# Opening of a two-block transformer kernel: the load of x moved to the head of SyncE's queue, and seven of the sixteen modulation pieces multiplied by TensorE instead of one

## The reference

```
c_act = silu(c)                                  # 1024 numbers
mod   = c_act @ w_ada + b_ada                    # w_ada is 1024 x 9216
sh1, sc1, g1, sh2, ... = split(mod, 9)
u = rmsnorm(x, norm_ff1) * (1 + sc1) + sh1
h = x + 0.5 * g1 * (silu(u @ w_gate) * (u @ w_up)) @ w_down
```

## Time and profile before

| | |
|---|---|
| median of 3 runs | 1648.84 us (1647.54 to 1648.98) |
| the profiled execution | 1650.04 us |
| its span | 1648.4 us |
| TensorE busy | 1624.7 us, 99% |
| VectorE, ScalarE, GpSimd busy | 1155.3, 799.2, 172.4 us |
| mean DMA rate | 191 GB/s |

### The profile page before, as it was taken

How to read it: one execution, slowest core, us unless ns; L and a number is a source line. 1 busy time by engine, 2 the same in 40 slices (tenths; PEclk the granted TensorE clock), 3 DMA queues, 4 the chain that set the end, 5 groups by cost and what they waited for, 6 DMA issues and landing times.

```text
span 1648.4 us, 33761 instructions
## 1 busy us (share of the span) xinstructions
PE 1624.7 (99%) x13615; PEld 1586.4 (96%) x13615; DVE 1155.3 (70%) x1449; ACT 799.2 (48%) x973; POOL 172.4 (10%) x193
## 2 busy tenths in 40 slices
PE   6999999999999999999999999999999999999999
PEld 4999999999999999999999999999999999999999
DVE  6877789778766657666687866656665587776653
ACT  3444445355544445444565654445444465554432
POOL 1100114500000000000062200000000035200000
PEclk9999999999999999999999999999999999999999
DMA  9998896646666467665744566568665654456653
GB/s 332 310 314 246 249 329 213 219 151 188 183 190 181 140 190 202 183 173 160 227 130 128 153 177 181 158 177 215 191 179 152 203 182 128 129 161 191 169 159 113
DMA packets 501553, 315.62 MB, mean 191 GB/s; under 512 B 14815, under 2 KB 489674, under 8 KB 501450
## 3 DMA queue, kind: packets, MB, share of 16 engines
q1 hardware_dynamic: 491824, 282.33, 60.1%
q0 software_dynamic: 8496, 29.92, 5.2%
q10 hardware_dynamic: 1130, 1.90, 0.3%
HBM read 313.04 MB, written 1.05 MB: 191 GB/s over the span
## 4 chain that ended last, share of the span: by engine, by line
PE 69%; DVE 6%; ACT 1%; issue 1%; ACTq 0%; DVEq 0%
PE accs L1731 20%; PE accs L1733 20%; PE accs L1732 19%; DVE wlo L1061 1%; PE wide L1771 1%; PE accs L1771 1%; PE accs L1769 1%; PE wide L1769 1%; PE wide L1770 1%; PE accs L1770 1%; DVE wlo L1052 1%; ACT prob L870 1%; DVE intra L1418 0%; PE wide L1998 0%; DVE st_max L1431 0%
## 5 line engine op out<-in xcount | busy, mean ns | idle before, releaser
L1731 PE MATMUL accs<-uhi_shift,whi 128*128 128x256 f32 x2304 | 650.6, 282 | 3.0 <-DVE ulo L1103 1.2
L1733 PE MATMUL accs<-uhi_shift,wlo 128*128 128x256 f32 x2304 | 646.7, 281 | 0.0
L1732 PE MATMUL accs<-ulo,whi 128*128 128x256 f32 x2304 | 643.0, 279 | 0.0
L738 ACT CAST whi<-raw 128x2048 fp32r<-128x2048 f32 (+2 forms) x294 | 499.6, 1702 | 104.6 <-PE accs L1733 67.7
L1052 DVE TENSOR_TENSOR wlo<-raw,whi 128x2048 fp32r<-128x2048 f32 (+2 forms) x249 | 496.4, 2001 | 4.1 <-ACT gat L979 3.1
L1731 PEld LDWEIGHTS accs<-uhi_shift,whi 128*128 128x128 f32 x2304 | 433.0, 188 | 11.3 <-issue 5.2
L1732 PEld LDWEIGHTS accs<-ulo,whi 128*128 128x128 f32 x2304 | 434.7, 189 | 1.2 <-issue 1.2
L1733 PEld LDWEIGHTS accs<-uhi_shift,wlo 128*128 128x128 f32 x2304 | 432.9, 188 | 0.0
L1731 PE MATMUL accs<-hhi,whi 128*128 128x256 f32 x1120 | 316.9, 283 | 1.0 <-DVE wlo L1052 0.7
L1733 PE MATMUL accs<-hhi,wlo 128*128 128x256 f32 x1120 | 314.6, 281 | 0.0
L1732 PE MATMUL accs<-hlo,whi 128*128 128x256 f32 x1088 | 307.4, 283 | 0.0
(11 more groups left out here) (357 smaller groups left out, 2191.6 us busy)
## 6 DMA issues: line engine op xcount, KB each, us to landing
raw<-in_ffn_w_in SPq DMA_DIRECT2D x176, 512.0 KB, 5.1
in_turn<-in_w_ada POOLq DMA_DIRECT2D x56, 512.0 KB, 5.6
raw<-in_w_mix_in SPq DMA_DIRECT2D x52, 512.0 KB, 4.6
raw<-in_ffn_w_out SPq DMA_DIRECT2D x64, 384.0 KB, 3.6
raw<-in_w_ff_gate SPq DMA_DIRECT2D x44, 512.0 KB, 4.9
raw<-in_w_ff_up SPq DMA_DIRECT2D x44, 512.0 KB, 6.3
raw<-in_w_in SPq DMA_DIRECT2D x40, 512.0 KB, 5.1
raw<-in_ffn_w_out SPq DMA_DIRECT2D x64, 320.0 KB, 4.1
```

Source lines behind the costliest of these rows:

```text
L738: nc.scalar.copy(whi[:, n % RING, 0:cols], raw[:, n % RING, 0:cols]).then_inc(hi_ready, 1)
L1731: mm(dst, wh, xh, start=first, stop=False)
L1732: mm(dst, wh, xl, start=False, stop=False)
L1733: return mm(dst, wl, xh, start=False, stop=last)
```

## The change

x is issued by SP, ahead of the pieces, in place of ScalarE. `DIRECT` becomes a list: the first 3 pieces of the first half and the first 4 of the second are multiplied by TensorE, the other 5 and 4 by VectorE; `SUMMED = [5, 9]` are the counts of `early_step` behind each half. Tile 0 of the first half stands within the transposes of x, tiles 1 and 2 behind them, tiles 0 and 1 of the second half behind the first group, tiles 2 and 3 in `second_part`. Thirteen of the sixteen dummy calls go. VectorE's sums of the second half stand ahead of the second half of chunk 0's split. ScalarE casts chunk 1 behind the modulation of tiles 4 to 7 and in two halves, with a semaphore `hi_half` for the first. GpSimd's first loads wait for `early_step` 8 of 9.

```
-DIRECT = 1
+DIRECT = [3, 4]
+SUMMED = [KD - DIRECT[0], 2 * KD - sum(DIRECT)]
...
+            sp.dma_start(u[:].rearrange("p k t -> p (k t)").rearrange("p (a d) -> p a d", a=TT),
+                         a["x"][0].rearrange("(a p) d -> p a d", p=P)).then_inc(x_in, 16)
             for half_ in range(2):
                 for k in range(KD):
...
-            pool.wait_ge(early_step, 2 * KD - DIRECT - 2)
+            pool.wait_ge(early_step, SUMMED[1] - 1)
             ada_load(0)
             ada_load(1)
             pool.dma_start(mask_in, a["level_masks"]).then_inc(masks_in, 16)
...
+            def split_hi_by_halves(n):
+                act.wait_ge(landed[n % RING], 32 * (n // RING + 1))
+                act.wait_ge(chunk_used, n + 1)
+                for side in range(2):
+                    c = slice(side * COLS[n] // 2, (side + 1) * COLS[n] // 2)
+                    nc.scalar.copy(whi[:, n % RING, c], raw[:, n % RING, c]).then_inc(hi_ready if side else hi_half, 1)
...
-            act.dma_start(u[:].rearrange("p k t -> p (k t)").rearrange("p (a d) -> p a d", a=TT),
-                          a["x"][0].rearrange("(a p) d -> p a d", p=P)).then_inc(x_in, 16)
...
             norm("up0", range(4))
-            split_hi(1)
             norm("up0", range(4, KD))
+            split_hi_by_halves(1)
...
-                dve.wait_ge(hi_ready, n + 1)
+                if (n, side) == (1, 0):
+                    dve.wait_ge(hi_half, 1)
+                else:
+                    dve.wait_ge(hi_ready, n + 1)
...
-            for k in range(KD):
+            for k in range(DIRECT[0], KD):
                 early_sum_step(0, k)
...
             norm("up0", range(4), lambda: split_lo_half(0, 0))
+            for k in range(DIRECT[1], KD):
+                early_sum_step(1, k)
             split_lo_half(0, 1)
-            for k in range(DIRECT, KD):
-                early_sum_step(1, k)
             early_take(1)
...
             def second_part():
-                for k in range(DIRECT):
+                for k in range(2, DIRECT[1]):
                     early_tile(1, k)
-                keep_clock(7)
+                keep_clock(1)
                 early_group(1)
                 keep_clock(2)
                 chunk_in(0)
...
             for k in range(KD + 2):
+                if k == 5:
+                    pe.wait_ge(c_ready, 1)
+                    early_tile(0, 0)
...
             ins.then_inc(stat, 1)
+            early_tile(0, 1)
+            early_tile(0, 2)
...
-            pe.wait_ge(c_ready, 1)
-            keep_clock(3)
             early_group(0)
-            keep_clock(4)
+            early_tile(1, 0)
+            early_tile(1, 1)
             ffn(0)
```

More of the change, by code:

```diff
@@ L334, in build @@
         first_half = sem("first_half")
+        hi_half = sem("hi_half")
         early_step = sem("early_step")
@@ L1174, in early_sum_step @@
             def early_sum_step(half_, k):
-                dst, first = early_sum[half_], DIRECT if half_ else 0
+                dst, first = early_sum[half_], DIRECT[half_]
                 dve.wait_ge(early_landed[half_ * KD + k], 16)
@@ L1180, in early_sum_step @@
                 else:
-                    dve.wait_ge(early_step, half_ * KD + k - first)
+                    dve.wait_ge(early_step, half_ * SUMMED[0] + k - first)
                     ins = nc.vector.scalar_tensor_tensor(out=dst, in0=ada_half(half_, k), scalar=c_act[:, k:k + 1],
@@ L1847, in early_group @@
             def early_group(half_):
-                pe.wait_ge(early_step, KD if half_ == 0 else 2 * KD - DIRECT)
+                pe.wait_ge(early_step, SUMMED[half_])
                 for j in range(KD):
                     ins = mm(early_column(half_, j), early_sum[half_][:, j // 4, j % 4 * P:(j % 4 + 1) * P], ones[:, 0:1],
-                             start=half_ == 0, stop=half_ == 0 or j == KD - 1)
+                             start=False, stop=j == KD - 1)
                 ins.then_inc(early_mod, 1)
```

## The result

The changed kernel takes 1655.76 us (median of 6 runs, 1653.02 to 1658.89), the kernel before 1648.38 beside it (6 runs, 1646.87 to 1649.88). The ratio is 1.0042, with a 95% interval of 1.0032 to 1.0052: slower by 0.42%, where 0.26% faster was forecast. The profiled execution took 1654.77 us, its span is 1653.1; that is 4.7 us over the profiled execution before.

A forecast was written before the change was run, and what follows sets the result against it. VectorE's multiplying in the opening was taken as the bound, 7.4 us behind the transfers; TensorE's chunk 2 at 50.3 instead of 54.65 gains 4.35 us, and, 1.2 lower for the median, gives 1644.5 us, range 1643.2 to 1647.6.

The forecast's parts named there:

- What bounds the kernel: Opening, second half of the modulation: VectorE's multiplying is 7.4 us behind the transfers, which the change can win.
- A tile is 16 records in 1.84 us: TensorE's opening: each tile moved there costs 1.84 us, two tiles 3.6, partly in room left by removed dummies.
- rival B: TensorE's opening: it falls to its slow pace under one-column matmuls; 1649.5 to 1652.5 us, chance 0.08.
- x first: Start of TensorE's transposes: x ahead of the pieces starts them 5.0 us earlier, at 7.1, with no delay to the pieces.
- rival C: Opening loads: x early brings nothing or holds the pieces back, by 3.2 us; 1645.8 to 1647 us, chance 0.09.
- GpSimd's loads: Before chunk 2: issued about 32.7 us, they go ahead of chunk 2, which lands at 45.6 instead of 41.0.
- the push: Chunk 2's landing: GpSimd's earlier loads delay it by 4.6 us, bounds nothing to 8.7.
- The halves of chunk 1: ScalarE's cast of chunk 1, moved and cut in two, costs VectorE 0.5 to 0.6 us before chunk 2.
- The sum: TensorE's chunk 2 starts at 50.3 instead of 54.65, a gain of 4.35 us, with nothing lost afterwards.
- faster: Whole kernel: a time below 1645.5 us, told from no change by 0.2%, 3.3 us; chance 0.68.

The follow-up runs named there:

- e2: The kernel before with its 16 dummy calls made one column wide, four for each one: 1662.27 us against 1649.13, ratio 1.0077.
- e11: The changed kernel without its six added tiles, with one tile on TensorE and 16 dummy calls as before: 1647.68 us against 1648.28, ratio 0.9996.
- e12: The kernel before with only the four dummy calls between the first group and chunk 0 made narrow: 1648.89 us, one run.
- e4: The changed kernel with one first-half and three second-half tiles on TensorE and dummies put back beside them: 1647.61 us against 1649.13, ratio 0.9995.
- e3: The kernel before with x alone moved to the head of SP's queue: 1648.08 us against 1649.13, ratio 0.9996.
- e6: As e4, but GpSimd's first loads are issued only behind the second group: 1647.74 us, one run.
- e5: As e4, but the second half's one-column matmuls stand between chunk 0's wide ones, with four dummy calls behind the first group: 1650.1 us, ratio 1.001.
- e8: As e5, but ScalarE's cast of chunk 1 is whole and ahead of the modulated tiles again: 1651.23 us, ratio 1.0013.
- e10: The changed kernel with one first-half and two second-half tiles on TensorE and 13 dummy calls: 1649.83 us, ratio 1.0004.
- e1: The changed kernel with one wide dummy call behind each tile and group that TensorE multiplies alone: 1658.68 us, ratio 1.0053.

## Why the prediction was wrong

**What bounds the kernel: right.** VectorE was 7.4 us behind the landings; relieved, it waited (7.97 us ahead of the second take).

**The step that failed: "A tile is 16 records in 1.84 us", and the dummies that go at no cost.** I took a price measured among wide matmuls, 1.84 us, and used it for ten microseconds of nothing else. The dummies that the change removes were treated as room to be filled. The runs showed otherwise: with the narrow tiles in their place the clock went from 2.4 to 1.2 GHz at 21.5 us, the group took 3.0 us and not 1.9, and the next two tiles 6.96 and not 3.6. e2 (narrow dummies alone) and e11 (the change without the tiles) show it from two sides, and e12 fits. I had this as rival B and gave it 0.08, because the one row I had, a narrow stretch of 1.8 us with the pace whole, was counted against it. It was evidence for 1.8 us only.

The other row, the slow first matmuls beside a printed clock of 1.00, could have warned: the clock had no record there, and TensorE ran at its slow pace. So the 1.00 printed for the first microseconds was no measurement; of narrow work this row says nothing.

**Rival B was also priced too low.** It had the fall at 20.5 us (it was near 21.5), 1.4 and 2.9 us for the group and the two tiles (1.1 and 3.4) and 5.3 for the 24 matmuls (30.55 to 35.5, 5.0). But it took the later tiles, the dummy call and the group at full clock, and its own terms make the end of that group 36.1 + 1.4 + 2.9 + 5.3 - 3.0 = 42.7, not 42.3. The clock fell again at 38.5: the two later tiles took 4.07 us, one dummy call 2.05, the group 3.41, and the second take was at 44.7. Its up to 2.5 us for a slow second half did not come: from the take to chunk 2 it was 13.15 us against 12.60 before, which is the halves of chunk 1. So B named the cause and had the size at chunk 2 (up to 3.1 us, measured 3.2), but partly in the wrong place, which is luck. With the short fall near 213 us this makes 4.7 us between the two profiled executions. The medians lie 7.4 apart. The other 2.7 us are where the profiled executions lie in their kernels' spread: that of before is 1.7 us above its median, that of the changed kernel 1.0 below. The runs outside the profile show only their mean clock, 0.990 to 0.992 for all six of the changed kernel.

**The Trainium skill** (TensorE: Matmul & The Clock Gate, What's actually happening) says that the full clock is passed while the engine is seen busy. The profile counts TensorE busy for 4.00 of 4 us in windows at 0.50, so the profile's busy share does not tell which of the two levels is granted. The prediction said that no row shows whether one-column matmuls count; e2 is that row: with them in the place of the wide dummies the clock was 0.53 from 24 to 38 us, and TensorE was busy for 14.00 of these 14 us.

**x first: half right.** The transposes started at 7.80 and not at 7.1, since the constants came at 7.6, not at 6.8, beside x. I gave the pieces no delay; the last landed 1.7 us later in the changed kernel and 1.1 in e4 (33.7). That was rival C, smaller than its 3.2. And the 5.0 us to be won at the transposes rested on one late landing: with x in its old place they started at 12.09 in the trace of before, but at 11.28 in e2 and 11.09 in e12. e3 and e11 gain 1.7 to 1.9 us at chunk 2 all the same.

**GpSimd's loads: the landing right, its weight not.** The loads went out at 34.5 us (forecast 32.7), and chunk 2 landed at 45.0 (forecast 45.6); the push is 3.9 us between e6 and e4, against the 4.6 taken. But in e4 it costs nothing: VectorE's own chain ends later. Had VectorE taken the second half at 36.1 as forecast, 1.8 us before e4, its chain would reach chunk 2 at 46.5, level with the cast's end at 46.6; this is an estimate from e4's rows. Late next was not chunk 2 but the third piece for `in_turn`, which I had priced at nothing: VectorE waits 1.7 us for it in the changed kernel (0.4 before), 2.5 in e4, where TensorE then waits 0.74.

**The halves of chunk 1: right.** Forecast 0.5 to 0.6 us, measured 0.45 as a wait and 0.54 between e5 and e8.

**The sum, had the clock held.** e4 comes nearest: 3.6 of 4.35 us at chunk 2, 3.0 between the profiled executions, 1.5 between the medians. So even with the clock mostly kept, the forecast of "faster" would have rested on an effect that runs of this kernel barely tell from none. No kernel here did all seven tiles with the clock whole.

## What to carry to other kernels

Dummy matmuls can be more than filling: before a change removes them or puts other work in their place, ask whether the clock stays up under that work, and read the granted clock window by window, not the busy time. Here weight loads with one moving column kept TensorE busy in the profile while its clock fell, even with real matmuls between. Moving matrix-vector products to TensorE cost 7.4 us with six added tiles; with two or three added and dummies beside them the kernel was level with before (e10, e4), and no dose was shown to gain. And a duration read from a short stretch is a price for a short stretch.

## What the runs showed of the hardware

- Spreading six narrow records among every three wide matmuls did not hold the clock: 0.50 from 32 to 48 us in e5. One wide call of 0.9 us behind each narrow 1.8 us did not either (e1).
- A transfer moved ahead on one queue delayed a small one on another: with x first on SP's queue the constants released TensorE at 7.6 to 7.9 us in all eleven traces (7.79 in e3, which has no other change), with x on ScalarE's at 6.82 us before, 6.77 in e2 and 6.70 in e12.
